# Between the first experts and latent attention: rows scaled by ScalarE, shift and scale applied after the transpose

## The reference, cut to what matters

```python
y = hier_moe(tokens, *moe_params)                      # two experts per row, weighted
xc = xc + mod_c[5] * y[:b * ctx_len]...                # gated residual, context rows
xl = xl + mod_l[5] * y[b * ctx_len:]...                # gated residual, latent rows
# next layer
hl = modulate(rmsnorm(xl, norm_g[layer, 0]), mod_l[0], mod_l[1])
hc = modulate(rmsnorm(xc, norm_g[layer, 0]), mod_c[0], mod_c[1])
p = h @ w_in                                           # mla_project

def rmsnorm(x, g): return x * rsqrt(mean(x * x) + EPS) * g
def modulate(h, shift, scale): return h * (1.0 + scale) + shift
```

## Time and profile before

| | |
|---|---|
| median of 3 runs | 2263.54 us (2262.79 to 2265.9) |
| the profiled execution's own time | 2274.16 us, its span 2272.5 us |
| PE / DVE / ACT / POOL busy | 1754.1 / 707.5 / 427.1 / 278.2 us |
| granted PE clock, mean | 0.894 |
| this stage, first DVE operation on a row to the last copy | 1190.54 to 1248.28 us |

### The profile page before, as it was taken

How to read it: one execution, slowest core, us unless ns; L and a number is a source line. 1 busy time by engine, 2 the same in 40 slices (tenths; PEclk the granted TensorE clock), 3 DMA queues, 4 the chain that set the end, 5 groups by cost and what they waited for, 6 DMA issues and landing times. The chain is left out here.

```text
span 2272.5 us, 26890 instructions
## 1 busy us (share of the span) xinstructions
PE 1754.1 (77%) x9482; PEld 971.1 (43%) x9483; DVE 707.5 (31%) x1277; ACT 427.1 (19%) x782; POOL 278.2 (12%) x355
## 2 busy tenths in 40 slices
PE   2559999979669878998642899999965889965651
PEld 0125444565434434344321546888543334433330
DVE  1130578563411211111117216555341111111114
ACT  3000144311001110101113114444200111111112
POOL 1030235121010100000014020000011000000001
PEclk9779999989779999999875899999977899988785
DMA  9971119510389999999963202000139999999993
GB/s 369 422 269 58 37 37 275 178 50 32 141 337 362 398 414 409 423 405 403 409 273 145 80 2 84 1 1 1 41 131 385 400 411 414 408 407 412 409 420 139
DMA packets 103369, 567.64 MB, mean 250 GB/s; under 512 B 21017, under 2 KB 39193, under 8 KB 63225
## 3 DMA queue, kind: packets, MB, share of 16 engines
q1 hardware_dynamic: 89152, 519.23, 57.3%
q0 software_dynamic: 7744, 26.22, 3.3%
q10 hardware_dynamic: 6392, 21.12, 2.4%
HBM read 525.02 MB, written 41.52 MB: 249 GB/s over the span
## 5 line engine op out<-in xcount | busy, mean ns | idle before, releaser
L1824 PE MATMUL exp_gps<-moew_wg,all_hT 128*64 128x512 f32 (+1 forms) x480 | 241.1, 627 | 29.7 <-DMA moew_wu<-in_moe_w_up 27.4
L1818 PE MATMUL exp_gps<-moew_wg,all_hT 128*32 128x256 f32 x1088 | 162.1, 462 | 101.1 <-DMA moew_wu<-in_moe_w_up 92.9
L1825 PE MATMUL exp_ups<-moew_wu,all_hT 128*64 128x512 f32 (+1 forms) x480 | 239.5, 623 | 0.0
L577 PE MATMUL abp_ps<-abp_w,all_hT 128*128 128x512 f32 x384 | 166.8, 593 | 0.9 <-PE abp_ps L577 0.6
L1818 PE MATMUL exp_ups<-moew_wu,all_hT 128*32 128x256 f32 x1088 | 161.1, 462 | 0.0
L1818 PEld LDWEIGHTS exp_gps<-moew_wg,all_hT 128*32 128x32 f32 x1088 | 81.3, 132 | 179.0 <-issue 137.3
L1824 PEld LDWEIGHTS exp_gps<-moew_wg,all_hT 128*64 128x64 f32 (+1 forms) x480 | 78.3, 167 | 166.7 <-issue 166.7
L1852 PE MATMUL exp_yps<-moew_wd,all_hT 128*64 128x512 f32 (+1 forms) x240 | 120.8, 621 | 20.4 <-issue 20.4
L1944 DVE TENSOR_TENSOR all_hT<-all_hT,exp_ups 64x512 f32<-64x512 f32 (+1 forms) x30 | 20.7, 690 | 340.7 <-ACT all_hT L1894 340.7
L215 PE MATMUL ada_ps<-ada_w,ada_sT 128*32 128x512 f32 x384 | 66.0, 850 | 76.1 <-DMA ada_w<-in_ada_w 76.1
L1854 PE MATMUL exp_yps<-moew_wd,all_hT 128*64 128x512 f32 (+1 forms) x240 | 120.3, 619 | 0.0
(11 more groups left out here) (384 smaller groups left out, 2555.8 us busy)
## 6 DMA issues: line engine op xcount, KB each, us to landing
moew_wg<-in_moe_w_gate SPq DMA_DIRECT2D x64, 2048.0 KB, 27.0
moew_wu<-in_moe_w_up SPq DMA_DIRECT2D x64, 2048.0 KB, 32.2
moew_wd<-in_moe_w_down SPq DMA_DIRECT2D x64, 2048.0 KB, 28.5
ada_w<-in_ada_w SPq DMA_DIRECT2D x12, 4096.0 KB, 25.5
abp_w<-in_ab_w_in SPq DMA_DIRECT2D x6, 2048.0 KB, 8.2
ys<-abp_zero SPq DMA_DIRECT2D x32, 384.0 KB
ys<-exp_y ACTq DMA_DIRECT2D x13, 512.0 KB
ys<-abp_zero SPq DMA_DIRECT2D x11, 512.0 KB
```

The costliest lines, as they stand in the source:

```text
L577: last = nc.tensor.matmul(ps[i % RB][:], hT[:, kk, what * P:(what + 1) * P], w[n % S][:, kk, :], start=(kk == 0), stop=(kk == KD - 1))
L1818: last = nc.tensor.matmul(bank[lo + j * Q:lo + (j + 1) * Q, 0:HC], x[:, k, 0:Q], wt[:, k, j * HC:(j + 1) * HC], start=(k == 0), stop=(k == ...
L1824: nc.tensor.matmul(gps[0:rows, :], x[:, k, 0:rows], w.g[q][:, k, :], start=(k == 0), stop=(k == KD - 1))
L1825: last = nc.tensor.matmul(ups[at:at + rows, :], x[:, k, 0:rows], w.u[q][:, k, :], start=(k == 0), stop=(k == KD - 1))
```

## The change

A function `combine_into_mla` takes the place of `combine` for layer 0 (the last `combine` is as before). What it does differently: DVE no longer writes `h`. ACT multiplies the row by `rstd` into `xn` (L2250), PE transposes that, ACT copies the first bank (L2244) and DVE the second (L2263) to `c.hT`. There a column of `h` is a partition, so `g * (1 + scale)` and shift are one number per partition and block: DVE makes them once on tiles of 128x8 (L2280), and `by_columns` applies both in place on `c.hT`, odd blocks on ACT (L2235), even ones on DVE (L2270), for the context half (256 wide) after turn 4 and for the latent half (512 wide) at the end. POOL does only the gathers (L2219). SP loads gains, shift and scale as columns, five loads of 1024 single floats each, right behind the gates and ahead of its wait for the first gathered pair (L2204, L2208); DVE waits for all five before its first row operation.

```diff
         def _(sp):
             load_gates(sp, c, gate, gate_ready, layer, 1, 2)
+            sp.dma_start(gcol[:], a["norm_g"][1, 0].rearrange("(k p) -> p k", p=P),
+                         allow_slow_non_contiguous=True).then_inc(cols_ready, 16)
+            for st in range(2):
+                for i in range(2):
+                    sp.dma_start(cols[:, st, i, :], c.mods[st, 1, i * DM:(i + 1) * DM].rearrange("(k p) -> p k", p=P),
+                                 allow_slow_non_contiguous=True).then_inc(cols_ready, 16)
             sp.wait_ge(got[0], 32)
-            norm.load(sp)
             prefetch(sp)
...
+        # scalar
+            def by_columns(half):
+                st, o, m = PARTS[half]
+                act.wait_ge(cols_done, 2)
+                act.wait_ge(ev_act, (o + m) // P)
+                act.wait_ge(ev_dve, (o + m) // P)
+                for kk in range(1, KD, 2):
+                    nc.scalar.activation(c.hT[:, kk, o:o + m], c.hT[:, kk, o:o + m], ACT.Identity,
+                                         scale=cols[:, st, 1, kk:kk + 1], bias=cols[:, st, 0, kk:kk + 1]).then_inc(aff, 1)
             for t in range(T + 2):
                 if t < T:
                     act.wait_ge(got[t % YB], 32 * (t // YB + 1))
                     nc.scalar.mul(y[t % YB][0][:], y[t % YB][0][:], r.w[:, 0, t:t + 1]).then_inc(weighed, 1)
+                if t >= 2:
+                    act.wait_ge(tr, 2 * (t - 2) + 1)
+                    nc.scalar.copy(c.hT[:, 0:4, (t - 2) * P:(t - 1) * P], tp[2 * (t % 2)][:]).then_inc(ev_act, 1)
                 if 1 <= t <= T:
                     norm.square(act, t - 1)
+                    act.wait_ge(rstd_done, t)
+                    if t >= 3:
+                        act.wait_ge(tr, 2 * (t - 3) + 2)
+                    nc.scalar.mul(xn[(t - 1) % 2][:], c.X[:, t - 1, :], norm.rstd[:, t - 1:t]).then_inc(scaled, 1)
-                if t >= 2:
-                    norm.first_half(act, t - 2)
-                    norm.second_half(act, t - 2, nc.scalar.copy)
+                if t == CT + 2:
+                    by_columns(0)
+            by_columns(1)
...
+        # vector, before the loop
+            dve.wait_ge(cols_ready, 16 * 5)
+            for st in range(2):
+                V.scalar_tensor_tensor(out=cols[:, st, 1, :], in0=cols[:, st, 1, :], scalar=1.0, in1=gcol[:],
+                                       op0=ALU.add, op1=ALU.mult).then_inc(cols_done, 1)
             for t in range(T + 2):
...                                                    # the three row operations on tile t as before
-                if t == 1:
-                    norm.prepare(dve)
                 if 1 <= t <= T:
-                    norm.scale(dve, link, t - 1)
+                    norm.inverse(dve, link, t - 1)
+                    dve.sem_inc(rstd_done, 1)
+                if t >= 2:
+                    evict(t - 2)
+                if t == CT + 2:
+                    by_columns(0)
+            by_columns(1)
```

More of the change, by code:

```diff
@@ L2102, in combine @@
         tile_done = lambda eng, t: eng.wait_ge(x_done, t + 1)
[L2103 to L2106, removed]
+        norm = FinalNorm(nc, c, a, s, t0, tile_done)
         block = s.block()
@@ L2277, in backbone @@
             k = mla_buffers(s1)
-            combine(nc, c, a, 0, 0, r, lambda sp: load_w_in(sp, a, k))
+            combine_into_mla(nc, c, a, r, lambda sp: load_w_in(sp, a, k))
             mla_layer(nc, c, a, k)
```

89 lines of the change are left out of this document (added).

## The result

| | before | after |
|---|---|---|
| median | 2263.54 us (2262.52 to 2271.3, 7 runs) | 2271.54 us (2268.46 to 2273.92, 7 runs) |
| ratio, 95% interval | | 1.0028 [1.0015, 1.0042] |
| timed again (first experiment) | 2267.9 us (2260.06 to 2274.26, 28 runs) | 2269.3 us (2264.05 to 2274.09, 12 runs) |
| ratio, 95% interval | | 1.0007 [0.9994, 1.002] |
| the profiled execution: own time, span | 2274.16, 2272.5 us | 2268.46, 2266.8 us |

The forecast was 2264.0, no change. The median of the first timing lies 1.0 us above the range, and its ratio puts the kernel 0.28% above before, with an interval that excludes no change. The second timing puts it at 0.07%, with no change inside the interval. The two profiles of the changed kernel show the stage no longer than before.

What follows compares the result with a forecast made beforehand. The bound was taken as DVE's program order (40.18 us), then a serial tail of 17.58 us. Turns and tail -7.0, later start +7.4 gave +0.4 us: 2264.0 us, range 2256.5 to 2270.5.

Steps and rivals of the forecast that it cites:

- stall of the gate multiply gone: DVE's gate multiply, 3.25 us beside POOL's shift, would take 1.23 us in all six turns.
- a turn: One turn of DVE in the loop would take 7.3 us, 0.8 less than the 8.09 before.
- context columns on the ring: In turn 4, ACT's four 256-wide column operations before weighting y(5) would add 1.3 us.
- the ring: DVE's chain, semaphore, ACT's scaling, then ACT's next weighting before DVE's next turn: 4.86 + 0.1 + 1.05 + 1.30 = 7.3 us.
- first row operation to the last turn: From DVE's first row operation to its last turn's start: 34.2 us against 40.18, 6.0 less.
- tail: From the last turn's start to the stage's end: 16.6 us against 17.56, 1.0 less.
- first row operation later by: DVE's first row operation would wait for the 5120 single floats and come 7.4 us later.
- sum in the stage: Turns and tail -7.0 us, later start +7.4 us: +0.4 us in all.
- Columns under the gathers: Rival at the stage's start: all 5120 floats pass by 1193, DVE starts at 1190.5 to 1192; 2257.2 us; chance 0.24.
- Descriptors as the bound: Rival at the start: slow descriptor generation, DVE's first row operation later than 1202; 2268.6 to 2273.0 us; chance 0.18.
- The turn that doesn't shorten: Rival in the loop: the ring is 7.8 us and the columns cost 2, +3.1, 2266.6 us; no separate chance.
- the microsecond that was named: Sign: if latent attention's first block changes by more than a microsecond, a term is missing.

Runs made afterwards that it cites:

- first experiment: The changed kernel timed and profiled once more, nothing changed: 2269.3 us against 2267.9 for the kernel before, ratio 1.0007.
- the run where PE was idle for only 0.38 us: The kernel before with POOL's shift left out in this stage, so h lacks the shift: 2253.06 us, ratio 0.994.

## Why the prediction was right, and where not

| step | forecast | measured |
|---|---|---|
| stall of the gate multiply gone | 3.25 to 1.23 | 1.22 in all six turns |
| a turn | 7.3 us | 7.15 us, three times |
| context columns on the ring | 1.3 | 9.12 - 7.15 = 1.97 |
| first row operation to the last turn | 34.2 | 34.29 |
| tail | 16.6 | 17.43 |
| first row operation later by | 7.4 | 5.55 |
| sum in the stage | +0.4 | -6.02 + 5.55 = -0.47 |

**The turn.** Right in mechanism and size, and the experiment with the weighting ahead shows that the ring was what held it: without that order the turn is 5.6, the lower end that was given. The kernel without the shift shows the stall's 2.02 us by itself.

**The columns on ACT.** The term was mis-sized. I priced a 256-wide operation by another kind of activation at no more than 0.42 and a 512-wide one by a copy at 0.58. Groups of the changed kernel by line and shape, busy us and mean ns:

```profile
L2235 ACT ACTIVATE all_hT<-all_hT,comb_cols 128x512 f32<-128x512 f32 x4 | 2.9, 802 | 1.1 <-DVE all_hT L2263 1.1
L2235 ACT ACTIVATE all_hT<-all_hT,comb_cols 128x256 f32<-128x256 f32 x4 | 2.1, 587 | 0.0
L2270 DVE TENSOR_SCALAR all_hT<-all_hT,comb_cols 128x512 f32<-128x512 f32 x4 | 1.9, 542 | 0.1
L2270 DVE TENSOR_SCALAR all_hT<-all_hT,comb_cols 128x256 f32<-128x256 f32 x4 | 1.4, 412 | 0.0
```

They cost 2.06 and 2.93 us in series instead of 1.3 and 2.1. That is 0.7 in the loop, offset there by turns shorter than forecast, and 0.8 in the tail, all of the gain that I gave it but 0.1. DVE's four ended at 1241.4, ACT's at 1242.4.

**The start.** The place and the wait were right, and two of its three terms were off. The last gathered rows came 13.7 us behind the gates' issue, not 15.0. (The prediction put only the gates beside the gathers of before; there the broadcast rows, issued from 1189.17, shared with the last of them too.) By then more single floats had passed than I took. Transfers by queue, packets, MB and share, 1180 to 1185 us, and 1186.3 to 1190.3, behind the gathers:

```profile
q0 software_dynamic: 525, 1.91, 97.1%
q1 hardware_dynamic: 604, 0.01, 7.7%
```

```profile
DMA packets 3096, 0.14 MB, mean 35 GB/s; under 512 B 3057, under 2 KB 3057, under 8 KB 3096
```

Beside the rows it was 1.15 to one, nearly the one-for-one of the earlier trace rows; but the loads also ran before the gathers filled the queues, so that about 5120 - 3057 = 2060 were through at 1186.3 where I had 505. By the Trainium skill ("DMA: Bandwidth & Descriptors", Queues, rings and completion order) an engine drains 9 to 17 descriptors of one ring before it turns to the next; the trace does not bear it out for these two queues. Equal counts alone would fit batches of equal length as well, but of the 94 single floats of the earlier trace rows 80 start about 6 ns ahead of a 4 KB row packet, so the two alternate. The prediction also read that rule wrongly. Taken for both queues alike, it lets about one float by for each row too, and would not finish the columns inside the gathers.

The rest went at 3057 / 4.0 = 764 a us in the mean, where I took 1062. That is 4.0 us instead of 4.3: more floats were through and the others went slower, two errors of opposite sign, which is luck. And the mean is no rate. The same 4.0 us in three windows, 1186.3 to 1187.5, to 1189 and to 1190.3:

```profile
DMA packets 1685, 0.07 MB, mean 57 GB/s; under 512 B 1670, under 2 KB 1670, under 8 KB 1685
DMA packets 339, 0.01 MB, mean 6 GB/s; under 512 B 337, under 2 KB 337, under 8 KB 339
DMA packets 1072, 0.06 MB, mean 49 GB/s; under 512 B 1050, under 2 KB 1050, under 8 KB 1072
```

There were 1670 single floats in 1.2 us, then 337 in 1.5, then 1050 in 1.3. In the thin stretch SP was still issuing the fifth load, until 1188.52, and that load's 1024 floats went behind it. The columns were there 1.82 us after SP's issue ended. In the repeat of the changed kernel the parts differ: the gathers ended 15.0 us behind the gates' issue, the other floats took 3.2 us. But there too the columns came 1.84 us after the end of SP's issue (1188.36), and 18.16 us after the gates' issue, against 17.74. So the sum repeats and its parts don't, and what came last was the issue of the fifth load. What held that issue, the gathers or the making of so many descriptors, no run separates.

So 15.0 + 4.3 + 0.6 = 19.9 became 13.7 + 4.0 + 0.35 = 18.05, with 18.09 measured.

**The rivals.** Columns under the gathers: refuted, 3057 packets were left. Descriptors as the bound: refuted as put, the start was 18.09 and not beyond 24. Yet its mechanism shows in part: SP was held for 13.80 us, and the 337 floats in 1.5 us, 225 a us, are fewer than the 344 of the earlier trace rows by which this rival was priced. They went so for 1.5 us and not for the whole rest. The turn that doesn't shorten: refuted at 7.15, though its 2 us for the columns were right.

**The stages behind.** Latent attention's first block took 10.26 us against 10.02, within the microsecond that was named. No large term is missing there; from latent attention's first load to the second layer's first expert weights the two profiles of the changed kernel take 440.57 and 440.60 us, the one of before 439.88.

**The sum.** It says no change, and the stage shows it twice, -0.47 and -0.03 us. That it came so close is luck in part: the turns and the tail gave 6.02 us and not 7.0, the start cost 5.55 and not 7.4, and the two errors offset each other. The median of the first timing is 8 us above before all the same. Of this the traces name 0.7 us at most, in latent attention: the profiled executions of the changed kernel are 5.7 and 8.6 us shorter in span than the one of before, and that difference lies in stages with the same code. The second timing, with more runs, gives 1.4 us. Whether the changed program is slower by a few us outside the stage stays open, and so does the same question for the kernel with the five loads added.

## What to carry to other kernels

When work leaves the engine that bounds a stage, look for the ring that the new order of waits closes: here 9.9 us of DVE's work and a wait of 3.64 us for broadcast rows went, and 7.4 us of waits for ACT came, which putting one weighting ahead of one wait took away (the loop went from 34.30 to 27.33 us). A per-column vector is loaded as contiguous rows and turned by PE; as single floats 20 KB cost 5.9 us at the head of a stage, where the six gathers beside them moved 3.1 MB. A load added to a kernel is priced only in the kernel where it will stand, because a wait that is already there can hide it.

## What was not expected of the hardware

An ACT operation with a scale and a bias per partition, in place in SBUF, took 0.80 us at 128x512 and 0.59 at 128x256, against 0.58 for a 512-wide copy out of PSUM; DVE's form with two scalars per partition took 0.54 and 0.41. Behind the gathers 3057 single floats took 4.0 us, in two bursts with a thin stretch of 1.5 us between them, and four loads of them held the issuing queue for 13.80 us (two loads 8.52). PE's granted clock, at 1.2 GHz through this stage before and after the change, rose ahead of the barrier in the run where PE was idle for only 0.38 us between the two last groups of eight transposes: 0.50 in the first group, 0.65 in the second, 1.00 behind them. Latent attention's first block took 8.00 us there. With 2.37 us idle between them (before) or 3.6 (the runs with the weighting ahead) the clock did not rise, and in all other runs that block took 9.44 to 11.04 us.
